# A weight ring of five 4 MB areas, filled in 2 MB halves, in place of eight 2 MB areas

## The reference

```python
for e in range(N_EXPERTS):                       # 32
    hdn = xt @ w1[e] + b1[e]
    gate = jnp.minimum(hdn[:, :D_FF_EXPERT], SWIGLU_LIMIT)
    up = jnp.clip(hdn[:, D_FF_EXPERT:], -SWIGLU_LIMIT, SWIGLU_LIMIT)
    act = (up + 1.0) * gate * jax.nn.sigmoid(SWIGLU_ALPHA * gate)
    out = out + combine[:, e:e + 1] * (act @ w2[e] + b2[e])
...
gate = jax.nn.sigmoid(rmsnorm(h, g_ple[l]) @ w_pg[l] + b_pg[l])
h = h + gate * (p[l] @ w_pp[l])
```

## Time and profile before

| | |
|---|---|
| time, median of 3 runs (lowest to highest) | 1099.24 us (1096.77 to 1099.93) |
| the profiled execution's own time | 1099.61 us |
| its span | 1097.9 us |
| PE busy | 1043.5 us (95%) |
| DVE busy | 386.0 us (35%) |
| ACT busy | 153.9 us (14%) |
| moved by DMA | 426.75 MB, mean 389 GB/s over the span |
| largest idle time of PE by cause | 22.9 us ahead of L1593, ended by the DMA of weights into `ring` |

### The profile page before, as it was taken

One profiled execution on the slowest core, in us unless ns is written; L12 is line 12 of the kernel. 1 busy time (PEld: TensorE's weight loads), 2 busy tenths in 40 slices (PEclk: granted clock), 3 DMA queues, 4 the chain that ended last, 5 costly groups with the idle time before them and its releaser, 6 DMA issues.

```text
span 1097.9 us, 15991 instructions
## 1 busy us (share of the span) xinstructions
PE 1043.5 (95%) x6374; PEld 434.4 (40%) x6374; DVE 386.0 (35%) x879; ACT 153.9 (14%) x268; POOL 12.6 (1%) x20
## 2 busy tenths in 40 slices
PE   9999999999999999999999999899999999999996
PEld 7884433333333333333333333233333333333332
DVE  6563743233333333333332222233333323332236
ACT  2560600101000000000000000000000000000034
POOL 0100200000000000000000000000000000000000
PEclk9999999999999999999999999999999999999998
DMA  9955599999999999999999999999999999999941
GB/s 292 354 190 206 208 388 427 428 429 429 427 425 427 429 428 430 427 429 429 427 429 428 428 428 429 430 429 427 426 429 429 429 429 429 427 427 427 426 173 40
DMA packets 40136, 426.75 MB, mean 389 GB/s; under 512 B 6216, under 2 KB 7444, under 8 KB 15536
## 3 DMA queue, kind: packets, MB, share of 16 engines
q1 hardware_dynamic: 40112, 426.41, 93.1%
HBM read 424.57 MB, written 1.43 MB: 388 GB/s over the span
## 4 chain that ended last, share of the span: by engine, by line
PE 65%; DMA 31%; DVE 3%; issue 1%; ACT 0%; DVEq 0%; SPq 0%
DMA ring<-in_w 31%; PE bank L1593 25%; PE bank L1634 14%; PE bank L1308 5%; PE bank L1526 3%; PE bank L1396 3%; PE bank L1536 3%; PE bank L1544 2%; PE bank L1683 1%; PE bank L1692 1%; DVE h L1110 1%; PE bank L1621 1%; PE bank L1580 1%; PE bank L1242 1%; PE bank L1615 1%
## 5 line engine op out<-in xcount | busy, mean ns | idle before, releaser
L1593 PE MATMUL bank<-ring,xgT 128*64 128x512 f32 x1536 | 341.0, 594 | 22.9 <-DMA ring<-in_w 22.9
L1593 PEld LDWEIGHTS bank<-ring,xgT 128*64 128x64 f32 x1536 | 106.7, 137 | 236.3 <-issue 183.8
L1634 PE MATMUL bank<-ring,actT 128*64 128x512 f32 x768 | 170.1, 595 | 0.0
L1152 DVE TENSOR_SCALAR gmin<-bank 128x512 f32<-128x512 f32 x32 | 22.1, 692 | 377.4 <-PE bank L1593 377.4
L1146 DVE TENSOR_SCALAR wpick<-slot_no,pos,share 128x128 f32<-128x128 f32 (+1 forms) x96 | 27.1, 339 | 229.5 <-PE bank L1593 229.5
L1634 PEld LDWEIGHTS bank<-ring,actT 128*64 128x64 f32 x768 | 53.0, 137 | 116.5 <-issue 101.9
L698 ACT ACTIVATE sig<-gmin 128x512 f32<-128x512 f32 x32 | 20.1, 630 | 484.8 <-DVE gmin L1152 484.8
L1110 DVE TENSOR_TENSOR h<-bank,h 128x512 f32<-128x512 f32 x132 | 84.8, 684 | 8.4 <-PE bank L1536 7.3
L1536 PE MATMUL bank<-y,wpickT 64*128 64x512 f32 x264 | 65.6, 615 | 0.8 <-ACT y L705 0.8
L1526 PEld LDWEIGHTS bank<-pick,x_parts 128*128 128x128 bf16 x1584 | 55.9, 98 | 25.5 <-issue 24.7
L1593 PE MATMUL bank<-far,xgT 128*64 128x512 f32 x256 | 57.9, 594 | 6.2 <-DMA far<-in_w 6.2
(11 more groups left out here) (296 smaller groups left out, 724.5 us busy)
## 6 DMA issues: line engine op xcount, KB each, us to landing
ring<-in_w SPq DMA_DIRECT2D x144, 2048.0 KB, 31.0
far<-in_w SPq DMA_DIRECT2D x24, 2048.0 KB, 32.5
hn_nT<-in_w SPq DMA_DIRECT2D x24, 2048.0 KB, 31.0
ring<-in_w_in SPq DMA_DIRECT2D x3, 2048.0 KB, 11.9
ring<-in_w_out SPq DMA_DIRECT2D x1, 4096.0 KB, 15.8
ring<-in_w_pg SPq DMA_DIRECT2D x4, 1024.0 KB, 28.5
h<-in_x_prompt SPq DMA_DIRECT2D x2, 512.0 KB, 3.9
ring<-in_w_in SPq DMA_DIRECT2D x2, 512.0 KB, 7.3
```

Of the source, the lines that this page charges most:

```text
L1152: dve.tensor_scalar(gmin[:], bank[0][:], LIMIT, None, ALU.min).then_inc(gmin_ready, 1)
L1593: ins = pe.matmul(bank[part][r, :], xgT[:, k, :], w[:, c:c + HALF], start=False, stop=(k == W1_SLOTS - 1), skip_group_check=True)
L1634: ins = pe.matmul(bank[2][CAP * m:CAP * (m + 1), :], actT[:, half:half + CAP], pair[:, c:c + HALF], start=(f == 0), stop=(f == FF // P - 1 ...
```

## The change

The memory map is written out by hand. The ring becomes five areas of 4 MB (`AREAS = 5`), 20 MB, at fixed addresses, and everything that the mixers need only for themselves lies in areas 2 to 4; tensors of the tail lie in areas 1 to 3. An expert now takes three areas: two for `w1` (each 512 rows, four consecutive rows or 32 KB to each partition) and one for `w2`. An area is filled by two DMAs of 2 MB (`load_half`): of `w1` a half is two of the partition's four rows, so 16 KB at a distance of 32 KB in HBM; of `w2` it is 512 consecutive rows as before. Each half has its own semaphore, and each waits for the two slots beneath it.

Ahead of the loop ten halves are issued in place of eight pairs: three after projections as before; one after the last; both of `w2` when the first sums of squares for mixer A are made (`yass_made`); one after `wout_late`; two after `mixed_made`; the tenth when the router's product is made and the samples' parts are through ScalarE (`xs_h`). `w_pp` goes ahead of the two `w2` halves, in two DMAs with pieces of 512 bytes.

The loop has a period of five steps: five written out, a loop over five times five, and two more (the last without a gather). The gather always stands after the scatter. Its weights now have a step of four bfloat16 columns (it was two), since four rows of `w1` lie in a partition. `embed_samples` moves from ahead of the loop to the end of step 2, and is transposed: 16 matmuls with 8 columns each; `embed` becomes four groups of eight matmuls with 128 columns, two after step 2 and two after step 3. The samples' part is turned back in the tail by eight transposes between L1408 and L1692. `bpg` and `gfin` are loaded right behind `w_pg`. Activations are worked out in place (`uclip`, `gmin`), and the share of each token is written to `share` directly.

```diff
-    AREAS, PERIOD = 8, 4
+    AREAS, FOUR, QUADS, W1_QUADS = 5, 4, SLOTS // 4, W1_SLOTS // 4
+    PERIOD = AREAS
+    LAST = NE % PERIOD
...
-        ring = sb("ring", [P, SLOTS, FF2])
-        hn_nT = sb("hn_nT", [P, NT * D + KD * T])
-        far = sb("far", [P, 2 * FF2])
+        ring = at(RING, "ring", [P, AREAS * FOUR, FF2])
+        area = [ring[:, FOUR * s:FOUR * (s + 1), :].rearrange("p s n -> p (s n)") for s in range(AREAS)]
...
-        x_pairs = x_parts[:].rearrange("p a t (j r q) -> p a t j r q", r=P, q=2)
+        x_quads = x_parts[:].rearrange("p a t (j r q) -> p a t j r q", r=P, q=FOUR)
...
+            def load_half(r, j, e, part):
+
+                s = (QUADS * r + j) % AREAS
+                if j < W1_QUADS:
+                    src = a["w1"][0][bass.ds(e, 1)][:, FOUR * j * P:FOUR * (j + 1) * P, :].rearrange(
+                        "e (p q) n -> p (e q n)", q=FOUR)
+                    cols = slice(2 * part * FF2, 2 * (part + 1) * FF2)
+                    dst, src = area[s][:, cols], src[:, cols]
                 else:
+                    src = a["w2"][0][bass.ds(e, 1)][:, FOUR * part * P:FOUR * (part + 1) * P, :].rearrange(
+                        "e (p q) n -> p (e q n)", q=FOUR)
+                    dst = area[s][:, 2 * part * FF2:2 * (part + 1) * FF2]
+                sp.dma_start(dst, src).then_inc(half_in[s][part], 16)
...
             sp.wait_ge(z_made, 4 * NB)
-            load_pair(0, W1_PAIRS - 1, 0)
-            load_pair(1, 1, 1)
-            sp.wait_ge(yarstd_made, GROUPS)
-            load(w_pp[:], a["w_pp"][0].rearrange("(k p) n -> p k n", p=P), wpp_in)
+            load_half(0, 1, 0, 1)
+            sp.wait_ge(news_ready, 1)
+            for k in range(PLE // P):
+                load(w_pp[:, :, k, :], a["w_pp"][0][k * P:(k + 1) * P, :].rearrange("p (b n) -> p b n", n=P), wpp_in)
+            sp.wait_ge(yass_made, 1)
+            for part in range(2):
+                load_half(0, 2, 0, part)
             sp.wait_ge(wout_late, 1)
-            load_pair(0, PAIRS - 1, 0)
+            load_half(1, 0, 1, 1)
             sp.wait_ge(mixed_made, NT)
-            load_pair(0, W1_PAIRS, 0)
+            load_half(1, 0, 1, 0)
+            load_half(1, 1, 1, 0)
             sp.wait_ge(b1_placed, 16 * 4 * PARTS)
+            sp.wait_ge(stored, 16 * 6)
             sp.wait_ge(logits_made, 1)
             sp.wait_ge(xs_low_ready, 2)
-            load_pair(1, 0, 1)
+            sp.wait_ge(xs_h, 3)
+            load_half(1, 1, 1, 1)
...
+            def refill(earlier, more, r, j):
+
+                s, g = (QUADS * r + j) % AREAS, QUADS * (PERIOD * more + r) + j - AREAS
+                e = (earlier * PERIOD + (PERIOD * more + r)) % NE
+                for part in range(2):
+                    sp.wait_ge(slots_free, earlier * (PERIOD * SLOTS) + (FOUR * g + 2 * part + 2))
+                    load_half(r, j, e, part)
...
-            embed_samples(0)
...
-            embed_samples(1).then_inc(pw_made, 1)
...
+                for b in range(KD):
+                    for k in range(PLE // P):
+                        ins = pe.matmul(bank[EMBED_BANKS[1]][:, b * NS:(b + 1) * NS], w_pp[:, b, k, :], pT[:, k, SEQ:T],
+                                        start=(k == 0), stop=(k == PLE // P - 1), skip_group_check=True)
...
+            def embed(g):
+
+                for b in (2 * g, 2 * g + 1):
+                    for t in range(2):
+                        c = (2 * (b - 2 * g) + t) * P
+                        for k in range(PLE // P):
+                            ins = pe.matmul(bank[EMBED_BANKS[g % 2]][:, c:c + P], pT[:, k, t * P:(t + 1) * P], w_pp[:, b, k, :],
...
-                    if k == W1_SLOTS - 2 and phase == PERIOD - 1:
-                        gather(i + 1)
...
-                if phase < PERIOD - 1:
+                if not (tail and phase == LAST - 1):
                     gather(i + 1)
...
                 if r in EMBED_STEPS:
                     pe.wait_ge(h_added, r * 2 * NT + NT + 4)
-                    embed(EMBED_STEPS.index(r))
+                    if r == EMBED_STEPS[0]:
+                        pe.wait_ge(wpp_in, 32)
+                        embed_samples()
+                    g = 2 * EMBED_STEPS.index(r)
+                    embed(g)
+                    pe.wait_ge(pw_ready, 1 + g)
+                    embed(g + 1)
...
             small_tile(bank[GATE_BANKS[2]], lambda k: tail_nT[:, k, SEQ:T], w_pg, range(KD)).then_inc(plegate_made, 1)
+            for b in range(KD):
+                ins = pe.transpose(bank[6 + b // 4][0:NS, (b % 4) * P:(b % 4 + 1) * P], pwT_samples[:, b, :], ident[:])
+            ins.then_inc(samples_back, 1)
```

More of the change, by code:

```diff
@@ L59, in decode_step, with at, row @@
     W_IN_CUTS = (0, 2, 4, KD)
-    AREAS, PERIOD = 8, 4
     EMBED_STEPS = (2, 3)
     WARM_UP = (5, 2)
-    EMBED_BANKS = ((6, 7), (6, 7), (1, 1))
+    EMBED_BANKS = (6, 7)
+    EMBED_BLOCKS, EMBED_GROUPS = KD, KD // 2
     PARTS = 3
     with ExitStack() as ctx:
-        def sb(name, shape, dt=F32, stack=ctx):
-            return stack.enter_context(nc.sbuf_tensor(name, shape, dt))
+        SIZE = {F32: 4, I32: 4, BF16: 2}
+        def at(offset, name, shape, dt=F32):
+            return nc.alloc_sbuf_tensor_at(name, shape, dt, offset=offset)
+        where = {}
+        def row(offset, end, *specs):
+            tensors = []
+            for name, shape, *dt in specs:
+                dt = dt[0] if dt else F32
+                tensors.append(at(offset, name, shape, dt))
+                where[name] = offset
+                words = 1
+                for n in shape[1:]:
+                    words *= n
+                offset += -(-words * SIZE[dt] // 32) * 32
+            assert offset <= end, (offset, end)
+            return tensors
         def sem(name):
@@ L98, in decode_step @@
[L98 to L110, removed]
@@ new lines, in decode_step @@
+        (h, b1_parts, y, ident, ones_b, before_b, slot_no, expert_pick, vecT, pos, share, eps_col, sumsq, squares,
+         table_junk, rms, rstd, n_steps, x_parts, xs_parts, pT, gmin, uclip, sig, actT, xgT, pick, wpick, wpickT,
+         b1_pick, top, picked_b, ex, negmax, exsum, rounds, head_sum, group_sum, pw, _) = lasting
+        GMIN, SIG, XGT, PARTS_AT, PW = [where[name] for name in ("gmin", "sig", "xgT", "x_parts", "pw")]
+        lg, left, br_row = row(PW, PW + 4 * 2 * P, ("lg", [P, NT, NE + TOP_K]), ("left", [P, NT, NE + TOP_K]),
+                               ("br_row", [P, NE]))
@@ new lines, in decode_step @@
+        rstd_rows, b1_wide = rstd_rows[:], b1_wide[:]
+        b1_cut = at(PARTS_AT, "b1_cut", [P, PARTS, HALF], BF16)
+        ws_both = at(GMIN, "ws_both", [P, 2, GROUPS, P])
+        wab, wxb = row(SIG, SIG + 4096, ("wab", [P, NB, P]), ("wxb", [P, NB, P]))
+        rest = (at(GMIN, "rest0", [P, D]), at(SIG, "rest1", [P, D]))
+        w_in = [at(in_ring(2 * g), f"w_in{g}", [P, KD, DL]) for g in range(4)]
+        xc, ug, rg, ig, decay, th, conv, vrows, news, w00, w00_diag, vss = row(
+            in_ring(2 * FOUR), in_ring(3 * FOUR),
+            ("xc", [P, NB, T]), ("ug", [P, NB, T]), ("rg", [P, NB, T]), ("ig", [P, NB, T]), ("decay", [P, NB, T]),
+            ("th", [P, NB, T]), ("conv", [P, NB, SEQ + 4 * NS]), ("vrows", [N_VECTOR_ROWS, P]), ("news", [P, NB, 36]),
+            ("w00", [P, GROUPS]), ("w00_diag", [P, GROUPS, NS]), ("vss", [P, NT, GROUPS]))
@@ new lines, in _ @@
+            load_half(1, 1, 1, 1)
[5 more added lines that the diff above has]
+                    load_half(r, j, e, part)
+            for r in range(1, PERIOD):
+                for j in range(2 if r == 1 else 0, QUADS):
+                    refill(0, 0, r, j)
@@ new lines, in _ @@
+            sp.wait_ge(steps_ready, 1)
+            blocks = sp.value_load(n_steps[0:1, 2:3], min_val=BLOCKS[0] - 1, max_val=BLOCKS[-1] - 1)
+            with sp.Fori(0, blocks) as i:
+                for r in range(PERIOD):
+                    for j in range(QUADS):
+                        refill(i, 1, r, j)
+            for r in range(LAST):
+                for j in range(QUADS):
+                    refill(blocks, 1, r, j)
+            sp.wait_ge(slots_free, blocks * (PERIOD * SLOTS) + (PERIOD + LAST - 1) * SLOTS)
```

372 lines of the change are left out of this document (154 added, 218 removed).

## The result

The changed kernel takes 1101.70 us (median of 12 runs, 1098.46 to 1103.26), the kernel before 1099.17 us on the same chip (12 runs, 1096.77 to 1100.02). The ratio is 1.0023, 95% interval 1.0015 to 1.0032. The forecast was 1089.8 us, so 11.9 us are missing.

What follows compares the result with a forecast made beforehand. The prediction took the DMA weight stream as the bound, with some 50 us of TensorE's time spare. Terms -9.8 - 0.5 + 0.9 = -9.4 us took the median 1099.24 to 1089.8 us; range 1087.3 to 1096.0.

Steps and rivals of the forecast that it cites:

- The larger ring: Ahead of the loop: ten loads in place of eight bring the same load 2 x 4.9 us sooner, -9.8 us.
- Rival D: Ahead of the loop: only one of the two extra loads falls into idle time, 1094.7 us; chance 0.03.
- The start of the loop: Before the first gather: two calls of `embed_samples` go, at most 0.15 us won, taken as 0.
- rival A: Queue runs dry early: embedding at upper price, tenth load late or slower clock at start; 1092 to 1096 us, chance 0.16.
- The embedding: After steps 2 and 3: 6.0 us (to 8.7) and 3.6 (to 4.4), hidden; taken 0, upper bound 3.0.
- The gather's weights: In each step's gather: reading at a step of 8 bytes costs 0 to 3.9 us a step, taken 0.
- Rival C: In the loop: the gather's weight loads make TensorE the bound, 1176 us; chance 0.04.
- The halves of `w1`: In the weight stream: 16 KB pieces 32 KB apart, taken at no loss; 1% slower would cost 5.9 us.
- rival B: In the weight stream: `w1` halves 32 KB apart stream more slowly, 1107 us at 3%; chance 0.07.
- The end: Last step and tail: the gather that goes wins 0.5 us, eight transposes of the samples cost 0.9 us.

Runs made afterwards that it cites:

- fix10: Changed kernel with contiguous `w1` halves, 8 and 7 idle matmuls at the start and the embedding one step later, loop of five kept; 1097.11 us.
- two_parts: fix10 with the third part (lowest bits) of the token tiles left out of the gather, 40 matmuls in place of 56 a step; 1090.33 us.
- after_two: Changed kernel with one edit, the third part left out of the gather (40 matmuls in place of 56 a step); 1091.18 us.
- lean_eight: Changed kernel with the gather cut to its first part, no samples, and the ninth and tenth load held back until two slots are free; 1101.41 us.
- ring9: fix10 with a ring of nine 2 MB halves in place of ten and a loop of three steps, nothing left out; 1093.39 us.
- a_warm: Changed kernel with 8 and 7 idle matmuls of 128 columns where `embed_samples` stood ahead of the loop; 1099.14 us.
- parts48: fix10 with the third part left out of the gather for the second token tile alone, 48 matmuls in place of 56 a step; 1096.92 us.
- a_contig: Changed kernel with each `w1` half read as contiguous rows and the gather's weights at a step of two columns again; 1100.25 us.
- b_p8: Kernel before with eight steps written out and a loop of eight in place of four and four; 1105.27 us.

## Why the prediction was wrong

**The step that failed** is the one that isn't there. The change was costed by what it does to loads, matmuls and waits; that the loop goes from four written-out steps to five was told and priced at nothing, without a word on what hides the code. Its price is 6.8 us where all else is mended (fix10 against two_parts) and 9.6 us in the changed kernel (against after_two). A small part of these two figures is the shorter gather itself. It is paid in the very resource that the prediction found to be the bound: the DMA engines. TensorE's stands are not the whole of it: in fix10 it again waits for data through the loop (26.6 us in 25 waits from 300 to 1000 us), and the time is still lost.

**The larger ring, -9.8 us:** right in mechanism and size (lean_eight 10.2 for two loads, ring9 5.1 for one). The tenth load was issued at 127.17 us in the trace of the changed kernel, and at 127.75 to 129.92 in those of the eight other kernels with ten loads ahead; the prediction took 129.8. Rival D falls.

**The start of the loop, 0:** wrong in part. The prediction named the fall of the clock under A and held against it that the gap was shorter than that of the earlier trace rows. The gaps were 2.45 and 1.76 us, with small matmuls between, and the granted clock from 126 to 132 us was 0.50; it fell within the first gap, over which its mean is 0.84. Keeping it up brought about 2 us (a_warm), though the intervals of the two ratios overlap (up to 1.0022 and from 1.0015).

**The embedding, 0:** mis-sized. The term for step 2 was 6.0 us with an upper price of 8.7; it took 9.0. The prediction put the whole shortfall between 0 and 3.0 us, and the queue lost 2.9. So rival A was true, at the places that the prediction named (holes near 225 and 254 us), but at 3 us it alone would have left the time inside the range.

**The gather's weights, 0:** right at the end, 0.2 us a step on TensorE. The Trainium skill's rule in SBUF — State Buffer (Door 1: The DMA port swizzle), by which eight bfloat16 columns of distance are free, doesn't hold for these weight loads (117 ns against 98). Rival C falls.

**The halves of `w1`:** right, rival B falls (298.25 MB with either layout). The loss that the Trainium skill tells of in DMA: Bandwidth & Descriptors (Latency and other measured facts) for rows a large power of two apart isn't seen at 32 KB.

**The end:** right. The transposes of the samples took 0.97 us, 0.9 was said. The last pair of `w1` starts at 1033.19 us, right when its load is in (992.95 + 40.20 = 1033.15), so the 0.5 us of the gather that went are won.

**The chances:** the cases held 0.07 for slower and 0.05 for no change, and every one was a variant of what the text had listed. The forecast of 1089.8 us was the time of a kernel without the fetches: two_parts, with all mended, has 1090.33 us. That the two lie so close is in part luck: against the kernel before on its chip two_parts gains 8.1 us, 9.4 were forecast.

What stays open: why the second stand at a turn (5.2 us) is missing, or at most 1.0 us, in the three kernels with idle matmuls and fetches, a_warm, fix10 and parts48, where the first one (1.9 to 2.6 us) remains; the idle matmuls shift the code by some 30 records, but that wasn't tried by itself. And which DMA engines carry the code: the views give the mean over 16 alone, so that the uneven end comes from the fetches is inferred from its going with them. It shows in the traces of all six kernels with fetches (changed, a_contig, a_warm, fix10, parts48, b_p8) and in none of the seven without.

## What to carry to other kernels

A step written out more often is a cost like a load or a matmul: count the matmuls and weight loads of one turn of the loop, and look at the instruction queue's line on the page. If its bytes grow with the number of turns, the turn is too long, and where DMA is the bound the fetches are paid in time (here more than their bytes would take). A ring whose period is short (here nine halves, three steps) can be worth more than a larger one with a long period.

## What the runs showed of the hardware

- Between 1610 and 1670 matmul and weight-load records a turn, TensorE's loop stops running in place: about ten packets of 16 KB more for each turn (40 more in four), a stand of 1.8 to 2.7 us at the branch and in two kernels (changed, a_contig) 3.9 to 5.2 us more shortly after.
- From 300 to 1000 us, 0.65 MB of code more went with 1.57 MB of weights less (changed against before; 0.59 with 1.43 MB in fix10 against two_parts): a packet of code costs the stream more than its bytes.
- After 7.6 us in which TensorE did four matmuls the granted clock was 0.50; a `w1` part right behind took 15.29 us in place of 13.73.
- Weight loads of bfloat16 at a step of 8 bytes take 117 ns, at 4 bytes 98.
